# A residual stream handed on times the sublayer root, in a one-core encoder kernel

## The chip, the cores and the metric

The kernel runs on one core of a Trainium2 chip. The metric is the device time of one launch in microseconds (us), smaller is better. The core's engines are TensorE (PE, with its weight loads shown apart as PEld), VectorE (DVE), ScalarE (ACT), GpSimd (POOL) and the queue of SyncE (SP) that issues the weight transfers.

## The reference

The reference is a two-layer encoder trunk over 272 tokens (16 meta tokens and 256 real ones) of width 1024. Six sublayers follow one another: FFN, attention, FFN in layer 0, FFN, a gated recurrent block, FFN in layer 1. Each is wrapped in two RMS norms:

```python
def rms_norm(x, g):
    return x * rsqrt(mean(x * x, axis=-1) + 1e-6) * g

h = h + 0.5 * rms_norm(swiglu(rms_norm(h, g[0]), w_in, w_out), g[1])
h = h + rms_norm(mixer(rms_norm(h, g[2])), g[3])     # attention or recurrent block
h = h + 0.5 * rms_norm(swiglu(rms_norm(h, g[4]), w_in, w_out), g[5])
```

After the last sublayer the 256 real tokens are returned.

## The kernel before

**Layout.** The stream `h` lies transposed, as 8 chunks of 128 features by 272 tokens (256 from the recurrent block's output on, where the meta tokens are dropped). A dense product is made in three TensorE products of split numbers: high weights times high input, low times high, high times low. So `xh` (ACT, `x_high`, line 989) and `xl` (DVE, `low_x`, L1414) are the high and low parts of `h` times the norm's gain, and `wh` (ACT, `high`, L983) and `wl` (DVE, `low`, L1408) those of a weight unit of 128 x 2048. The norm's factor over features is a number for each token; it is put on the products' outputs, as `r` (L1423).

**Order.** Everything is written out by hand, one queue for each engine, with semaphores between them. Weight units go through four slots: SP loads a unit once its slot's `w_ready` has come, ACT makes `wh`, DVE makes `wl`, TensorE uses both.

**The boundary between two sublayers.** There are five, numbered here first to fifth by `pj` = 0 to 4. The output projection leaves 8 tiles in PSUM. ACT squares each (`square_tile`, L1015, into `sqb`) and copies it times the gain into `mg` (L1017). DVE adds the squares of tiles 0 to 5 into `acc` (L1431). Then:

- `mean_of_projection` (TensorE): three products with `acc` and three with each of the two last squares give the mean square of each token, with 96 tokens in partitions (L633). Three products keep the array warm (L482).
- `root_of_projection` (ACT, L1024): the root of 96 x 3 numbers. DVE takes their reciprocal (L1441). TensorE spreads them over 128 partitions with 3 products (`spread`, L521), into the PSUM tile `SUM_POST`.
- `residual` (DVE): for each chunk, `mg` times `SUM_POST` (L1446), `h` plus `mg` (L1450), and, one chunk behind, `xl` (L1414).
- ACT makes `xh` and the square `sqh` of each chunk (L989, L996) and GpSimd sums the squares in `hacc` (`sum_squares`: a copy for the first, L1914, and seven additions, L1917).
- TensorE begins the next sublayer with `chunk`: for each of 8 chunks of `h`, eight products with `xh` (L490, L491) as soon as that is there, then four with `xl` (L493).
- `mean_of_h` (L528) makes the mean square of the new `h` from `hacc`; root (L1006), reciprocal (L1419), `spread_r` (L521) and the copy into `r` follow.

After the recurrent block DVE makes one more weight unit's low part (`low(U_FFN[3] + 2, 0)`) between `residual` and the next sublayer's first step.

**At the start** DVE copies the eight turned chunks of the input out of PSUM (L1868) between the first halves of weight units (L1854), and then makes the eight `xl`.

**At the end** `turn_h` and `copy_h` (L668, L1128) turn `h` to token rows while the last FFN runs.

## Time and profile before

| | |
|---|---|
| median of 3 runs | 1066.18 us (1065.68 to 1066.78) |
| the profiled execution | 1066.7 us |
| its span from first to last instruction | 1064.9 us |
| PE, PEld busy | 99%, 96% of the span |
| DVE, ACT, POOL busy | 64%, 52%, 8% of the span |
| mean granted TensorE clock | 0.999 of full speed |
| chain that ended last | PE 92%, DVE 4%, ACT 2%, DMA 1% |

What lies around the span is 1.8 us. Matmuls overlap in the pipeline, so the duration of one is longer than the step to the next.

### The profile page before, as it was taken

To read this page: it belongs to the slowest core of one execution; us is meant where nothing else is said; L and a number is where in the kernel's file an instruction comes from. 1 tells how busy PE (TensorE), PEld (TensorE's weight loads), DVE (VectorE), ACT (ScalarE), POOL (GpSimd) and SP (SyncE) were. 2 spreads that over 40 slices of the span, in tenths; PEclk is the share of its full clock that TensorE was granted. 3 is DMA by queue.
4 is the path that set the end of the run, shared out by engine and by line. 5 is a ranking of instruction groups with operands and counts; after the bars stand their busy time and mean duration, and the time that the engine had idled before them with its cause. 6 is when DMAs were issued, how large, how long until landed. Compare 5 with 4: busy or idle time off the path is not lost.

```text
span 1064.9 us, 20573 instructions
## 1 busy us (share of the span) xinstructions
PE 1050.2 (99%) x8400; PEld 1022.3 (96%) x8400; DVE 686.2 (64%) x994; ACT 551.4 (52%) x806; POOL 81.2 (8%) x84
## 2 busy tenths in 40 slices
PE   9999999999999999999999999999999999999997
PEld 8999999999779999999999999999999999999986
DVE  6666656478865866654467666644798668667652
ACT  5444454457775644435455444444579755454541
POOL 0000000028000100000020000000234210000000
PEclk9999999999999999999999999999999999999999
DMA  9564446625204345535644554466328426646541
GB/s 309 174 211 158 138 147 205 222 90 171 69 2 159 119 159 164 190 130 181 205 159 160 190 165 138 134 207 210 101 86 271 159 81 203 193 158 208 190 135 40
DMA packets 160911, 170.16 MB, mean 160 GB/s; under 512 B 3264, under 2 KB 154104, under 8 KB 160840
## 3 DMA queue, kind: packets, MB, share of 16 engines
q1 hardware_dynamic: 160456, 168.70, 49.0%
q8 instruction: 51, 0.84, 0.3%
q0 software_dynamic: 96, 0.28, 0.1%
q10 hardware_dynamic: 288, 0.18, 0.1%
q14 instruction: 20, 0.16, 0.1%
HBM read 167.82 MB, written 1.05 MB: 159 GB/s over the span
## 4 chain that ended last, share of the span: by engine, by line
PE 92%; DVE 4%; ACT 2%; DMA 1%; issue 0%; SPq 0%; DVEq 0%; ACTq 0%
PE bank L474 23%; PE bank L476 23%; PE bank L475 23%; PE bank L884 5%; PE bank L682 2%; PE bank L681 2%; PE bank L683 2%; PE bank L493 1%; PE bank L490 1%; PE bank L491 1%; PE weighed L788 1%; DVE xl L1414 1%; PE flipped L776 1%; DVE h L1450 1%; DMA raw<-in_rec_w_in 1%; PE bank L521 1%
## 5 line engine op out<-in xcount | busy, mean ns | idle before, releaser
L1408 DVE TENSOR_TENSOR wl<-raw,wh 128x2048 fp32r<-128x2048 f32 (+2 forms) x164 | 339.2, 2090 | 152.5 <-ACT wh L983 152.2
L474 PE MATMUL bank<-xh,wl 128*128 128x272 f32 (+1 forms) x1488 | 430.6, 289 | 3.4 <-DVE tmp L1478 1.1
L476 PE MATMUL bank<-xh,wh 128*128 128x272 f32 (+1 forms) x1488 | 427.4, 287 | 0.0
L475 PE MATMUL bank<-xl,wh 128*128 128x272 f32 (+1 forms) x1488 | 425.9, 286 | 0.0
L983 ACT ACTIVATE wh<-raw 128x2048 fp32r<-128x2048 f32 (+2 forms) x164 | 282.2, 1744 | 104.6 <-PE bank L476 82.9
L474 PEld LDWEIGHTS bank<-xh,wl 128*128 128x128 f32 x1488 | 280.4, 188 | 5.2 <-issue 2.7
L476 PEld LDWEIGHTS bank<-xh,wh 128*128 128x128 f32 x1488 | 280.4, 188 | 0.0
L475 PEld LDWEIGHTS bank<-xl,wh 128*128 128x128 f32 x1488 | 280.3, 188 | 0.0
L474 PE MATMUL bank<-ah,wl 128*128 128x272 f32 x528 | 152.2, 288 | 0.0
L475 PE MATMUL bank<-al,wh 128*128 128x272 f32 x528 | 152.0, 288 | 0.0
L476 PE MATMUL bank<-ah,wh 128*128 128x272 f32 x528 | 151.6, 287 | 0.0
L1050 ACT ACTIVATE tmp<-tmp 128x272 f32<-128x272 f32 (+1 forms) x88 | 37.7, 428 | 215.3 <-DVE tmp L1477 215.0
L475 PEld LDWEIGHTS bank<-al,wh 128*128 128x128 f32 x528 | 99.4, 188 | 0.0
L474 PEld LDWEIGHTS bank<-ah,wl 128*128 128x128 f32 x528 | 99.3, 188 | 0.0
L476 PEld LDWEIGHTS bank<-ah,wh 128*128 128x128 f32 x528 | 99.2, 188 | 0.0
L1496 DVE TENSOR_TENSOR al<-tmp,ah 128x272 f32 (+3 forms) x88 | 38.2, 438 | 51.0 <-ACT ah L1055 50.6
L1477 DVE TENSOR_TENSOR tmp<-bank,r 128x272 f32<-128x272 f32 (+1 forms) x88 | 38.1, 433 | 49.9 <-PE bank L476 49.8
L1055 ACT ACTIVATE ah<-tmp 128x272 f32 (+3 forms) x88 | 37.4, 428 | 47.4 <-DVE tmp L1486 47.4
L1914 POOL COPY hacc<-sqh 128x272 f32<-128x272 f32 (+1 forms) x5 | 2.4, 484 | 706.9 <-ACT sqh L996 706.9
L490 PE MATMUL bank<-xh,wl 128*128 128x272 f32 (+1 forms) x176 | 46.0, 289 | 1.9 <-ACT xh L989 1.7
L1486 DVE TENSOR_TENSOR tmp<-tmp 128x272 f32<-128x272 f32 (+1 forms) x88 | 38.2, 437 | 14.0 <-ACT tmp L1050 10.8
L491 PE MATMUL bank<-xh,wh 128*128 128x272 f32 (+1 forms) x176 | 45.5, 287 | 0.0
(205 smaller groups left out, 1197.1 us busy)
## 6 DMA issues: line engine op xcount, KB each, us to landing
raw<-in_ffn_w_in SPq DMA_DIRECT2D x88, 1024.0 KB, 5.4
raw<-in_ffn_w_out SPq DMA_DIRECT2D x24, 768.0 KB, 4.3
raw<-in_ffn_w_out SPq DMA_DIRECT2D x24, 640.0 KB, 3.9
raw<-in_ffn_w_out SPq DMA_DIRECT2D x10, 1024.0 KB, 5.1
raw<-in_rec_w_in SPq DMA_DIRECT2D x8, 1024.0 KB, 5.7
raw<-in_attn_w_qkv SPq DMA_DIRECT2D x6, 1024.0 KB, 5.0
raw<-in_attn_w_o SPq DMA_DIRECT2D x4, 1024.0 KB, 5.6
raw<-in_rec_gate_w SPq DMA_DIRECT2D x16, 256.0 KB, 5.1
```

Of the source, the lines that this page charges most:

```text
L474: pe.matmul(dst, b, mh, start=first, stop=False)
L475: pe.matmul(dst, a, ml, start=False, stop=False)
L476: return pe.matmul(dst, a, mh, start=False, stop=last)
L490: pe.matmul(dst, b, xh[:, k, t0:L], start=k == 0, stop=False)
L491: pe.matmul(dst, a, xh[:, k, t0:L], start=False, stop=False)
L884: done = pe.matmul(dst[:, cols], w, x[:, cols], start=first and half == 0, stop=last, skip_group_check=True)
L983: act.activation(wh[:, slot(u), 0:kn * 256], raw[:, slot(u), 0:kn * 256], ACT.Copy).then_inc(wh_ready, units)
L1050: act.activation(sl[:, b, t0:L], gp[:, b, t0:L], ACT.Silu).then_inc(silu_done, 1)
L1408: dve.tensor_tensor(wl[:, slot(u), 0:kn * 256], w, wh[:, slot(u), 0:kn * 256].bitcast(F32), ALU.subtract).then_inc(w_ready, units)
L1477: dve.tensor_tensor(gp[:, b, t0:L], bank[banks[0]][:, t0:L], r[:, t0:L], ALU.mult).then_inc(gate_scaled, 1)
L1486: dve.tensor_tensor(aa[:, b, t0:L], sl[:, b, t0:L], up[:, b, t0:L], ALU.mult).then_inc(a_full, 1)
L1496: dve.tensor_tensor(d, aa[:, b, t0:L], s, ALU.subtract).then_inc(a_ready, 1)
```

## The change

Where a sublayer gave h + p/root (p the projection times its gain, root the root mean square of the projection), it now hands on h*root + p, which is root times the true stream. The next norm takes the factor out again, as long as its epsilon is multiplied by root squared; ACT puts that into `hacc` ahead of the squares (`hacc_set`). The steps:

- The mean square is made in all 128 partitions at once: `exact` products of 128x128 mean weights with `acc` and with the square of tile 7; DVE adds the square of tile 6 too (`ACC` = 9). ACT takes the root of 128 x 272 numbers straight out of PSUM into the SBUF tile `root`. The reciprocal and the spread between them and `residual` are gone. All 9 warming products stand behind.
- `residual` multiplies `h` by `root` (both in SBUF) and adds `mg`.
- Later, in the next sublayer's output projection, DVE inverts `root` (`invert_root`, 128 x 272 reciprocals), and GpSimd multiplies the 8 chunks of `h` by it (`restore`), before the next boundary uses `h`. Four sublayers do that; in the last the factor is put on by ACT's copy in `copy_h`, from `root_tok`, which `spread_r` and DVE make.
- `mean_of_h` moves into the products behind the chunks: for attention into tile 4 (k == 1), for the last FFN into its third tile (k == 2), with `spread_r` there from k == 3 to k == 6.
- GpSimd's first step of `sum_squares` is an addition in place of a copy.
- At the start ACT copies chunks 5 to 7 of `h`, and DVE makes two `xl` ahead of a weight half.

```diff
+EPS_SCALE = float(np.sqrt(D // P * EPS))
-        ACC = 8
+        ACC = 9
             def spread_r(n):
                 pe.wait_ge(rc_ready, n + 1)
+                if n == 5:
+                    for t in range(2):
+                        pe.matmul(SUM_PRE[:, SC + 3 + t:SC + 4 + t], root[:, META + t * P:META + (t + 1) * P], ident[:, 0:1], start=True, stop=True)
                 spread(SUM_PRE, rc_pre).then_inc(r_spread, 1)
-                if n:
+                if n in (1, 2):
                     mean_of_h(X_OF_FFN[n])
-                            if n == 0 and f == f0 + 2 and part == 0 and k == 7:
-                                mean_of_h(0)
-                            if f == f0 + 2 and (part, k) == ((0, 3) if n else (1, 6)):
+                            if f == f0 + 2 and (part, k) == {0: (0, 7), 3: (0, 2)}.get(n):
+                                mean_of_h(X_OF_FFN[n])
+                            if f == f0 + 2 and (part, k) == {0: (1, 2), 3: (0, 6)}.get(n, (0, 3)):
                                 spread_r(X_OF_FFN[n])
             def mean_of_projection(pj):
-                first = True
-                for ready, value, squares in ((acc_step, ACC * pj + ACC, acc[:, :]),
-                                              (sq_ready, 8 * pj + 7, sqb[:, 0, :]), (sq_ready, 8 * pj + 8, sqb[:, 1, :])):
-                    pe.wait_ge(ready, value)
-                    for c, a in enumerate(KTOK):
-                        last = pe.matmul(SUM_POST[0:KT, SC + c:SC + c + 1], squares[:, a:a + KT], mean_w,
-                                         start=first, stop=value == 8 * pj + 8, skip_group_check=True)
-                        first = False
-                last.then_inc(post_sum, 1)
-                idle_bank = bank[3] if pj == 4 else bank[5]
-                keep_warm(3, idle_bank)
-                pe.wait_ge(rt_ready, pj + 1)
-                spread(SUM_POST, rc_post).then_inc(rt_spread, 1)
-                keep_warm(6, idle_bank)
+                a, w = PROJ_T0[pj], mean_w.broadcast_to([P, P])
+                pe.wait_ge(acc_step, ACC * pj + ACC)
+                exact(SUM_POST[:, a:L], w, acc[:, a:L], True, False)
+                pe.wait_ge(sq_ready, 8 * pj + 8)
+                exact(SUM_POST[:, a:L], w, sqb[:, 1, a:L], False, True).then_inc(post_sum, 1)
+                keep_warm(9, bank[3] if pj == 4 else bank[5])
...
-                mean_of_h(1)
...
+                            if k == 1:
+                                mean_of_h(1)
...
             def root_of_projection(pj):
+                a = PROJ_T0[pj]
                 act.wait_ge(post_sum, pj + 1)
-                act.activation(rc_post[:, :], SUM_POST[0:KT, SC:SC + 3], ACT.Sqrt, bias=EPS).then_inc(post_root, 1)
+                if pj:
+                    act.wait_ge(h_restored, 8 * pj)
+                act.activation(root[:, a:L], SUM_POST[:, a:L], ACT.Sqrt, bias=EPS).then_inc(post_root, 1)
+                act.wait_ge(post_root, pj + 1)
+                act.wait_ge(pre_sum, pj + 1)
+                act.activation(hacc[:, a:L], root[:, a:L], ACT.Square, scale=EPS_SCALE).then_inc(hacc_set, 1)
...
+                act.wait_ge(root_inverted, 5)
+                act.activation(h_tok[:, t, 512 * half:512 * half + 512], bank[6][:, :], ACT.Copy, scale=root_tok[:, t:t + 1]).then_inc(h_turned_copied, 1)
...
+            def invert_root(n):
+                dve.wait_ge(hacc_set, n)
+                dve.reciprocal(root[:, PROJ_T0[n]:L], root[:, PROJ_T0[n]:L]).then_inc(root_inverted, 1)
             def residual(pj):
                 n, t0 = pj + 1, PROJ_T0[pj]
+                if pj:
+                    dve.wait_ge(h_restored, 8 * pj)
+                dve.wait_ge(mg_ready, 8 * pj + 8)
                 dve.wait_ge(post_root, pj + 1)
-                dve.reciprocal(rc_post[:, :], rc_post[:, :]).then_inc(rt_ready, 1)
-                dve.wait_ge(mg_ready, 8 * pj + 8)
-                dve.wait_ge(rt_spread, pj + 1)
                 def scale(c):
-                    dve.tensor_tensor(mg[:, c, t0:L], mg[:, c, t0:L], SUM_POST[:, t0:L], ALU.mult).then_inc(mg_scaled, 1)
+                    dve.tensor_tensor(h[:, c, t0:L], h[:, c, t0:L], root[:, t0:L], ALU.mult).then_inc(h_scaled, 1)
...
                 def group(g, it=0):
                     for j in range(3):
+                        if (g, j) == (3, 2):
+                            add_squares(pj, 6)
                         next_unit(g, j, it)
...
                 group(0)
+                if n:
+                    invert_root(X_OF_FFN[n])
...
             def projection(pj, u0):
                 for g in range(4):
+                    add_squares(pj, 2 * g)
                     if g < 3:
-                        add_squares(pj, 2 * g)
                         add_squares(pj, 2 * g + 1)
                         low(u0 + g + 4, 0)
+                    if g == 0:
+                        invert_root(pj)
                 residual(pj)
...
             def recurrent_out():
-                for m in range(6):
+                invert_root(4)
+                for m in range(7):
                     add_squares(4, m)
...
             def sum_squares(n):
-                pool.wait_ge(pre_sum, n)
-                if n == 2:
-                    pool.wait_ge(norm_q_sum, 1)
+                pool.wait_ge(hacc_set, n)
...
+            def restore(n):
+                t0 = PROJ_T0[n]
+                pool.wait_ge(root_inverted, n)
+                pool.wait_ge(x_ready, 8 * n + 8)
+                for c in range(KC):
+                    pool.tensor_tensor(h[:, c, t0:L], h[:, c, t0:L], root[:, t0:L], ALU.mult).then_inc(h_restored, 1)
```

`restore(1)` stands behind GpSimd's `rotary`, `restore(2)` and `restore(3)` behind `sum_squares` of their number, `restore(4)` behind GpSimd's part of the recurrent block.

## Rows read from the trace of the kernel before

**Rows 1.** Stretches: us, busy PE, PEld, DVE, ACT, POOL (instructions), clock, DMA share, GB/s

```profile
343.00:356.00 13.00, 12.64 (x99) 12.35 (x99) 11.00 (x22) 8.28 (x17) 6.29 (x8) 1.00 0.01 2
356.00:545.00 189.00, 189.00 (x1510) 189.00 (x1509) 113.85 (x135) 87.35 (x103) 0.00 (x0) 1.00 0.54 177
```

**Rows 2.** Timeline of the second boundary: start, duration, engine, line [idle before <-releaser]

```profile
338.67 0.59 PE L633 MATMUL bank<-cst,acc 128*96 128x1 f32 x6
338.86 0.40 ACT L1015 ACTIVATE sqb<-bank 128x272 f32<-128x272 f32 x1 [2.25 <-PE bank L476]
...
339.12 1.16 PE L633 MATMUL bank<-cst,sqb 128*96 128x1 f32 x12
...
340.31 0.17 ACT L1024 ACTIVATE rc_post<-bank 96x3 f32<-96x3 f32 x1 [0.67 <-PE bank L633]
...
341.80 0.44 DVE L1446 TENSOR_TENSOR mg<-mg,bank 128x272 f32<-128x272 f32 x1 [1.12 <-PE bank L521]
```

**Rows 3.** Timeline of DVE in its residual, second boundary

```profile
344.69 1.01 DVE L1414 SCALAR_TENSOR_TENSOR xl<-h,vec_a,xh 128x272 fp32r<-128x272 f32 x1
345.63 0.42 DVE L1446 TENSOR_TENSOR mg<-mg,bank 128x272 f32<-128x272 f32 x1
346.09 0.73 DVE L1450 TENSOR_TENSOR h<-h,mg 128x272 f32<-128x272 f32 x1
346.74 0.49 DVE L1414 SCALAR_TENSOR_TENSOR xl<-h,vec_a,xh 128x272 fp32r<-128x272 f32 x1
...
353.92 0.50 DVE L1414 SCALAR_TENSOR_TENSOR xl<-h,vec_a,xh 128x272 fp32r<-128x272 f32 x1 [0.18 <-ACT xh L989]
```

**Rows 4.** Timeline of GpSimd in the same stretch

```profile
343.75 0.47 POOL L1914 COPY hacc<-sqh 128x272 f32<-128x272 f32 x1 [75.49 <-ACT sqh L996]
344.50 0.90 POOL L1917 TENSOR_TENSOR hacc<-hacc,sqh 128x272 f32<-128x272 f32 x1 [0.28 <-ACT sqh L996]
345.73 0.78 POOL L1917 TENSOR_TENSOR hacc<-hacc,sqh 128x272 f32<-128x272 f32 x1 [0.33 <-ACT sqh L996]
...
354.28 0.78 POOL L1917 TENSOR_TENSOR hacc<-hacc,sqh 128x272 f32<-128x272 f32 x1 [1.26 <-ACT sqh L996]
```

**Rows 5.** Timeline of TensorE: its first chunk product and what follows the last

```profile
343.42 0.36 PE L490 MATMUL bank<-xh,wl 128*128 128x272 f32 x1 [0.35 <-ACT xh L989]
...
355.89 0.59 PE L528 MATMUL bank<-cst,hacc 128*96 128x1 f32 x6
```

**Rows 6.** Chain that ended last: the two halves of one exact fp32 product of 272 columns

```profile
236.43 0.34 PE bank L738 x2
236.76 0.23 PE bank L739 x2
```

**Rows 7.** DVE groups by shape: busy us, mean ns of one

```profile
L1677 DVE RECIPROCAL rinv<-rsum 128x2 f32<-128x2 f32 x16 | 2.6, 160 | 1.2 <-ACT prow L1233 1.1
...
L1832 DVE RECIPROCAL small<-small 128x16 f32<-128x16 f32 x1 | 0.3, 253 | 0.0
```

**Rows 8.** Timeline of DVE in the first FFN's projection

```profile
174.05 1.76 DVE L1408 TENSOR_TENSOR wl<-raw,wh 128x1536 fp32r<-128x1536 f32 x1 [0.23 <-DVE qg L1844]
```

**Rows 9.** Timeline of TensorE where the attention's chunks end

```profile
233.33 0.59 PE L528 MATMUL bank<-cst,hacc 128*96 128x1 f32 x6
234.25 0.36 PE L474 MATMUL bank<-xh,wl 128*128 128x272 f32 x1 [0.33 <-ACT tmp L1174]
```

**Rows 10.** Chain that ended last, behind the fifth boundary's last chunk

```profile
879.28 2.77 DVE wl L1408
882.09 0.39 PE bank L474
```

**Rows 11.** Timeline of TensorE at the kernel's start, before the second unit's tiles

```profile
20.09 0.39 PE L490 MATMUL bank<-xh,wl 128*128 128x272 f32 x1 [0.16 <-DVE wl L1854]
```

**Rows 12.** Timeline of DVE and ACT in the recurrent block's output projection

```profile
850.88 4.48 DVE L1408 TENSOR_TENSOR wl<-raw,wh 128x2048 fp32r<-128x2048 f32 x2
...
864.19 0.38 ACT L1348 ACTIVATE sqb<-bank 128x256 f32<-128x256 f32 x1 [1.04 <-PE bank L884]
```

More of the change, by code:

```diff
@@ L189, in build @@
         rc_pre = sb("rc_pre", [KT, 3])
-        rc_post = sb("rc_post", [KT, 3])
+        root = sb("root", [P, L])
+        root_tok = sb("root_tok", [P, 2])
         rsq = sb("rsq", [KT, 3])
@@ L278, in build @@
             "gu_done", "gate_scaled", "silu_done", "up_scaled", "a_full", "ah_ready", "a_ready"))
-        proj_done, sq_ready, mg_ready, acc_step, post_sum, post_root, rt_ready, rt_spread, mg_scaled = (sem(n) for n in (
-            "proj_done", "sq_ready", "mg_ready", "acc_step", "post_sum", "post_root", "rt_ready", "rt_spread", "mg_scaled"))
+        proj_done, sq_ready, mg_ready, acc_step, post_sum, post_root, h_scaled, hacc_set, root_inverted, h_restored = (sem(n) for n in (
+            "proj_done", "sq_ready", "mg_ready", "acc_step", "post_sum", "post_root", "h_scaled", "hacc_set", "root_inverted", "h_restored"))
         qk_done, q_squared, q_gained, q_sum, q_step, q_root, q_rot, q_partner, q_cos, q_sin, q_roped, q_spread, q_final = (sem(n) for n in (
@@ L1005, in root_of_h @@
                 act.wait_ge(pre_sum, n + 1)
-                act.activation(rc_pre[:, :], SUM_PRE[0:KT, SC:SC + 3], ACT.Sqrt, bias=EPS).then_inc(pre_root, 1)
+                act.activation(rc_pre[:, :], SUM_PRE[0:KT, SC:SC + 3], ACT.Sqrt, bias=0.0 if n else EPS).then_inc(pre_root, 1)
             def square_tile(pj, m, b, it=0):
@@ L1127, in copy_h @@
                 act.wait_ge(h_turned, i + 1)
-                act.activation(h_tok[:, t, 512 * half:512 * half + 512], bank[6][:, :], ACT.Copy).then_inc(h_turned_copied, 1)
+                act.wait_ge(root_inverted, 5)
+                act.activation(h_tok[:, t, 512 * half:512 * half + 512], bank[6][:, :], ACT.Copy, scale=root_tok[:, t:t + 1]).then_inc(h_turned_copied, 1)
             def last_out():
@@ L1198, in attention @@
                 act.wait_ge(norm_q_sum, 1)
-                act.activation(rc_q[:, :], SUM_PRE[:, SC + 3:SC + 8], ACT.Sqrt, bias=EPS).then_inc(norm_q_root, 1)
+                act.activation(rc_q[:, :], SUM_PRE[:, SC + 3:SC + 8], ACT.Sqrt).then_inc(norm_q_root, 1)
                 root(0)
@@ L1373, in _ @@
             for c in range(5, KC):
+                act.wait_ge(x_trans, c + 1)
+                act.wait_ge(h_ready, c)
+                act.activation(h[:, c, :], bank[4 + c % 4][:, 0:L], ACT.Copy).then_inc(h_ready, 1)
                 x_high(0, c)
@@ L1465, in ffn @@
                 r_of_h(X_OF_FFN[n])
+                if n == 3:
+                    dve.reciprocal(root_tok[:, :], SUM_PRE[:, SC + 3:SC + 5]).then_inc(root_inverted, 1)
                 if n == 0:
@@ L1875, in _ @@
             low_half(0, 0)
-            for c in range(5, KC):
-                copy_h(c)
+            dve.wait_ge(vec_ready, 1)
+            low_x(0, 0)
+            low_x(0, 1)
             low_half(0, 1)
-            dve.wait_ge(vec_ready, 1)
-            for c in range(KC):
+            for c in range(2, KC):
                 low_x(0, c)
@@ L1907, in sum_squares @@
                 t0 = PROJ_T0[n - 1]
-                pool.wait_ge(pre_sum, n)
-                if n == 2:
-                    pool.wait_ge(norm_q_sum, 1)
+                pool.wait_ge(hacc_set, n)
                 for c in range(KC):
                     pool.wait_ge(hsq_ready, 8 * n + c + 1)
-                    if c == 0:
-                        pool.tensor_copy(hacc[:, t0:L], sqh[:, 0, t0:L]).then_inc(hacc_step, 1)
-                    else:
+                    if c:
                         pool.wait_ge(hacc_step, 8 * n + c)
-                        pool.tensor_tensor(hacc[:, t0:L], hacc[:, t0:L], sqh[:, c % 2, t0:L], ALU.add).then_inc(hacc_step, 1)
+                    pool.tensor_tensor(hacc[:, t0:L], hacc[:, t0:L], sqh[:, c % 2, t0:L], ALU.add).then_inc(hacc_step, 1)
+            def restore(n):
[4 more added lines that the diff above has]
+                    pool.tensor_tensor(h[:, c, t0:L], h[:, c, t0:L], root[:, t0:L], ALU.mult).then_inc(h_restored, 1)
             def rotary():
@@ L1975, in _ @@
             rotary()
+            restore(1)
             sum_squares(2)
+            restore(2)
             sum_squares(3)
+            restore(3)
             sum_squares(4)
             recurrent()
+            restore(4)
             sum_squares(5)
```

2 lines of the change are left out of this document (1 added, 1 removed).

## Prediction

> **What bounds the kernel.** I read the stretches first. Inside a sublayer TensorE is busy all the time (189.00 of 189.00 us from 356 to 545 at clock 1.00, while DVE has 75 us and ACT 102 us free) [rows 1]. Nothing that DVE, ACT or GpSimd gain or lose there shows in the time, as long as TensorE's inputs come before they are due. The time can only move where TensorE waits: at the kernel's start and at the five boundaries. So I went through the second boundary on the timeline (first, third and fourth have the same steps and durations within 0.1 us), and then through what differs at the first and the fifth.
>
> A boundary has two parts. In the first a single chain runs: the last square ends at 339.26, TensorE's mean products (nine, done in order, so the last square waits behind the sums before it) at 340.28, ACT's root at 340.48, and after reciprocal and spread DVE's first multiply starts at 341.80 [rows 2]. I call that moment T0. It is 2.54 us after the last square. In the second part DVE feeds TensorE chunk by chunk. TensorE begins at T0 + 1.62 and ends at T0 + 14.09 [rows 5]. Its 96 products at 0.126 us each (189.00 us over 1510) are 12.1 us [rows 1], so it waits only 0.4 us inside. DVE's last `xl` ends at T0 + 12.62 [rows 3]: that is 1.58 us a chunk against TensorE's 1.51, so the two are nearly even, and whichever grows is the bound.
>
> **What the second part is made of.** Undisturbed, DVE's three operations start 0.46 (multiply to add), 0.36 (add to `xl`) and 0.42 us (`xl` to the next multiply) apart, 1.24 us a chunk. But some are stretched: the `xl` at 344.69 takes 1.01 us where the one at 346.74 takes 0.49, and the add at 346.09 takes 0.73 where others take 0.44 [rows 3]. Each stretched one begins while a GpSimd addition runs (344.50, 345.73) [rows 4]. GpSimd lets it go at 344.69 + 0.52 = 345.21 and at 346.09 + 0.29 = 346.38, about 0.65 us after its own start (0.71 in the first case, where GpSimd itself had to wait for the add before). The multiply at 345.63 was not stretched, and no multiply is: one of its inputs lies in PSUM. Over the boundary six additions cost DVE 3 x 0.52 + 3 x 0.29 = 2.4 us, and in every second chunk part of GpSimd's time passed under the multiply.
>
> **The change, part by part.**
>
> *The chain to T0.* The last square ends at the same time and TensorE can take it at once (+0.06). One exact product of 272 columns takes 0.34 + 0.23 = 0.57 us [rows 6]. ACT then makes the root of 128 x 272 out of PSUM: like its square of the same shape, 0.40 us [rows 2], plus 0.04 and 0.03 us from engine to engine. Sum: 0.06 + 0.57 + 0.04 + 0.40 + 0.03 = 1.10 us where it was 2.54: T0 comes 1.4 us earlier. Bounds: if the root took what an `xh` takes (0.52), 1.3; if it were as short as the old root (0.17), 1.65. The new add of tile 6 lies beside TensorE's last tile; where it stands before a 2.29 us `low`, that ends some 0.5 us before T0. ACT's square for `hacc` falls in the 0.95 us before the first `xh`.
>
> *The chunks.* The multiply is now `h` times `root`, two inputs in SBUF, like the add and the `xl`. I take it that it is held up as they are. The first GpSimd step becomes an addition too. I follow the queues with these rules: the starts above; a DVE operation on two SBUF inputs keeps GpSimd out for 0.30 us; GpSimd keeps DVE out for 0.65 us; GpSimd's addition is due 1.41 us after the start of the add of its chunk. For the old kernel this gives the last `xl` at T0 + 12.73 and TensorE's end at T0 + 14.14 (trace: 12.62 and 14.09). For the new one seven additions hold up, in turn, a multiply by 0.54, an add by 0.48, an `xl` by 0.59, an add by 0.56, and so on: 3.8 us in all. The `xl` end at T0 + 2.15, 4.41, 6.24, 7.96, 9.79, 11.51, 13.34, 13.75; TensorE needs chunk 6's (13.34) + 0.06, then 0.50 for its rest and 1.51 for chunk 7: T0 + 15.41. DVE is now the bound at 1.78 us a chunk, and this part is 1.3 us longer. Bounds: no hold-up of the multiply, 0.07; GpSimd keeping 0.75 in place of 0.65, 2.2. The net of a boundary is 1.3 - 1.4 = -0.1 us.
>
> The Trainium skill, "SBUF — State Buffer", section "Who interferes with whom", says that a DVE instruction with two SBUF inputs contends with a GpSimd instruction that reads SBUF, and one with at most one SBUF input does not. That is the line that the rows show between `mg` and the other two, and it speaks against this change.
>
> *Third, fourth and second boundary.* Three times -0.1: -0.3 us.
>
> *First boundary.* The next tile waits for ACT (`q_gained`) and starts at 234.25, and the mean products at 233.33 lie in that gap [rows 9]. The start moves forward by some 0.2 us, but the mean products now stand inside the tile, where TensorE is never idle: six passes of 0.09 us, +0.55. Net +0.35.
>
> *Fifth boundary.* TensorE waits for a low weight part that DVE makes behind its last `xl`, until 882.09 [rows 10]. That comes 1.4 earlier and 1.0 later: -0.4. The mean products stood in that wait and now cost 0.55; `spread_r` has two more products with `root` (four passes, 0.37). Net +0.5. The next unit's low part, behind the reciprocal of the later root, is due only 0.15 us after it is ready: cover that could go, at up to 0.5 us.
>
> *Start.* TensorE misses 0.33 us before 20.09, waiting for DVE's half unit [rows 11]. DVE loses three copies (1.13 us); ACT takes them and has 0.8 us to spare. -0.3.
>
> *Inverting and restoring.* From 2 to 16 elements a reciprocal grows from 160 to 253 ns, 6.6 ns each [rows 7]: 272 make an estimated 1.95 us, four times. In the first FFN a string of small DVE operations (3.7 us) at the same place made the next `low` late, at 174.05 [rows 8], and TensorE missed nothing there. So it costs nothing. Eight GpSimd multiplies follow, at 0.71 us or so (its additions take 0.78 with overlap [rows 4]), 5.7 us in projections of 19 to 65 us. Nearest to late is the fifth boundary: DVE is free at 855.36, the inverse done at 857.3, the eight done by 863.0, or 865.1 if all seven DVE adds hold them up by 0.3; ACT's root wants them at 865.3 [rows 12]. Cover there is 0.2 to 2.3 us. Without it each us late is a us lost.
>
> **Sum.** -0.3 (start) + 0.35 (first) - 0.3 (second to fourth) + 0.5 (fifth) = +0.25 us on the profiled execution's 1066.7 (span 1064.9 and 1.8 around it), which lies 0.5 us above the median of the runs, 1066.18. On the median: **1066.4 us, no change**. Own range 1064.1 to 1068.3.
>
> **Rivals.**
>
> *A. The multiply is hardly held up.* GpSimd may slip behind DVE's now unbroken row of two-input operations, or the lock may not bite on this form. Then the whole 1.4 us of each boundary is kept: -0.3 - 7.0 + 0.55 + 0.92 = -5.8, 1060.4; with half of the hold-up, 1063.6. For it: between multiply and `xl` the gap is longer (0.12 us) and GpSimd's sum is not urgent. Against: the add and the `xl`, of the same kind, were held every time. 27%.
>
> *B. The restored stream comes late at the fifth boundary* (slower). If a GpSimd multiply takes 1.0 us, as wide ones with contention do, and the seven adds hold it up, it ends at 857.3 + 8.0 + 2.1 = 867.4, 2.1 us late: 1068.5. It decides from 0.8 us a multiply on. Against: 0.71 was seen free of DVE. 11%.
>
> *C. A GpSimd addition shuts DVE out for its whole recorded 0.78 us.* The same hand working gives T0 + 16.48 for TensorE's end: +1.0 at each boundary, 1072. Against: 0.65 fits the rows of the old kernel to 0.1 us. 5%.
> The Trainium skill, same page and section, says that the one that comes second fully blocks for the whole instruction; by that C would be the outcome, and the trace so far agrees only in part (0.52 and 0.29 of delay, by when the operation came).
>
> **Chances.** Forecast 52%, A 27%, B 11%, C 5%, 5% for a stall not seen (a late weight part at 885, a slower reciprocal). 0.2% is 2.1 us, about what this kernel's runs can tell from no change. Faster by more: A and a little of the forecast, 0.28. Slower: B, C and the rest in part, 0.17. Same: 0.55. Range 1061.8 to 1068.9: it leaves out A's end and C.
>
> **What would show it.** In the new trace: DVE's first multiply 1.1 us after the last square's end (step 1). Multiplies of 0.43 us and, every second chunk, of 0.9 us, and 1.78 us a chunk (step 2); if all multiplies take 0.43, A holds. TensorE's first chunk product to its last 13.8 us in place of 12.5. One reciprocal near 1.95 us in each of four sublayers, TensorE still fully busy there. The last of eight GpSimd multiplies before ACT's root; if ACT waits for it, B. The forecast fails if GpSimd's additions pass under the DVE row or behind it.

## The result, and the profile after

The changed kernel takes 1067.69 us (median of 19 executions, 1066.35 to 1070.67) against 1066.19 us of the kernel before (19, 1065.30 to 1066.78): ratio 1.0018, 95% interval 1.0012 to 1.0024. The forecast was 1066.4, no change beyond 0.2%. The median is 1.3 us above it, inside the stated range. Six of the 19 lie at 1068.99 to 1070.67, and all six have a mean granted clock of 0.996 or 0.997, the others 0.998 to 1.000; the median of these other thirteen is 1067.11. The profiled execution took 1067.87 us (span 1066.0, before 1064.9).

Part 1 of the page (busy time, share of the span, instructions) says only that TensorE is still the bound; the other engines have room:

```profile
PE 1049.9 (98%) x8324; PEld 1017.2 (95%) x8324; DVE 703.8 (66%) x996; ACT 556.2 (52%) x814; POOL 120.7 (11%) x116
```

Where the time moved is read by laying both timelines side by side at points that both kernels have: the end of each boundary's last square, and TensorE's first product behind the fifth boundary.

| point | before | after | after - before |
|---|---|---|---|
| last square, first boundary | 216.68 | 215.05 | -1.63 |
| second | 339.26 | 337.93 | -1.33 |
| third | 544.89 | 543.49 | -1.40 |
| fourth | 750.54 | 749.03 | -1.51 |
| fifth | 864.57 | 863.99 | -0.58 |
| TensorE goes on behind the fifth | 882.09 | 882.12 | +0.03 |
| end of the span | 1064.9 | 1066.0 | +1.1 |

So 1.6 us were won before the first boundary, little moved from there to the fourth, 0.9 were lost between the fourth and the fifth, 0.6 at the fifth boundary and 1.1 behind it. The fourth boundary itself is not where the 0.9 went: from its last square to the mean products of `h` (L528 before, L530 after) both kernels take 16.6 us. They went in the recurrent block.

The first row holds some chance. TensorE's first product with `xh`:

```profile
13.67 0.37 PE L508 MATMUL bank<-xh,wl 128*128 128x272 f32 x1
...
13.90 0.37 PE L510 MATMUL bank<-xh,wl 128*128 128x272 f32 x1
```

It starts at 13.67 before and at 13.90 after, and in the profiles of all the kernels here anywhere from 12.60 to 14.03, whatever was changed. What makes it vary is open; it lies in the idle products at the very start, which take 5.7 to 7.2 us. Counted from this product the first boundary's last square comes after 203.01 us before and after 201.15 us after, and in each of the nine other profiles of kernels with the change after 201.14 or 201.15. So the change won 1.86 us there, and this one profile gave 0.23 of them back.

The timeline of the second boundary after, by engine (start, duration, engine, line; idle before it and who ended it in brackets), answers to [rows 2 to 5]:

```profile
337.53 0.40 ACT L1012 ACTIVATE sqb<-bank 128x272 f32<-128x272 f32 x1 [2.25 <-PE bank L478]
338.75 0.40 ACT L1024 ACTIVATE root<-bank 128x272 f32<-128x272 f32 x1 [0.44 <-PE bank L881]
...
338.00 0.71 PE L881 MATMUL bank<-sqb,cst 128*128 128x136 f32 x4
...
339.27 0.44 DVE L1458 TENSOR_TENSOR h<-h,root 128x272 f32<-128x272 f32 x1 [1.90 <-ACT root L1024]
...
341.35 1.02 DVE L1458 TENSOR_TENSOR h<-h,root 128x272 f32<-128x272 f32 x1
342.41 0.89 DVE L1462 TENSOR_TENSOR h<-h,mg 128x272 f32<-128x272 f32 x1
...
344.46 1.01 DVE L1421 SCALAR_TENSOR_TENSOR xl<-h,vec_a,xh 128x272 fp32r<-128x272 f32 x1
345.39 0.43 DVE L1458 TENSOR_TENSOR h<-h,root 128x272 f32<-128x272 f32 x1
345.86 0.91 DVE L1462 TENSOR_TENSOR h<-h,mg 128x272 f32<-128x272 f32 x1
...
344.25 0.91 POOL L1934 TENSOR_TENSOR hacc<-hacc,sqh 128x272 f32<-128x272 f32 x1 [1.25 <-ACT sqh L993]
345.50 0.96 POOL L1934 TENSOR_TENSOR hacc<-hacc,sqh 128x272 f32<-128x272 f32 x1 [0.33 <-ACT sqh L993]
...
354.56 0.59 PE L530 MATMUL bank<-cst,hacc 128*96 128x1 f32 x6
```

T0 is 339.27, 1.34 us after the last square (it was 2.54), TensorE's last chunk product ends at T0 + 15.29 (it was 14.09). Of the multiplies only the one at 341.35 is stretched, by 0.59, and the add behind it by 0.45. From there on each pair of chunks has one `xl` stretched by 0.52 and one add by 0.46; before, the add lost 0.29 [rows 3]. The seven additions of GpSimd hold DVE up by 3.5 us in all.

The restoring work, in the second boundary's sublayer (DVE's inverse, then GpSimd's eight multiplies), and ahead of the fifth boundary:

```profile
324.49 1.85 DVE L1447 RECIPROCAL root<-root 128x272 f32<-128x272 f32 x1
...
326.42 10.67 POOL L1942 TENSOR_TENSOR h<-h,root 128x272 f32<-128x272 f32 x8 [59.49 <-DVE root L1447]
...
856.57 6.69 POOL L1942 TENSOR_TENSOR h<-h,root 128x256 f32<-128x256 f32 x8 [10.20 <-DVE root L1447]
```

The eight end at 337.09 and the root wants them at 338.75; at the fifth boundary [rows 12] they end at 863.26, wanted at 864.80. Cover is 1.5 to 1.7 us. One multiply takes 1.33 us on average in the second boundary's sublayer and 0.84 ahead of the fifth boundary, waits included.

Two things that the prediction did not have. In the first FFN of the kernel before, TensorE waited 1.11 us because DVE got `r` only at 33.36:

```profile
34.84 0.39 PE L474 MATMUL bank<-xh,wl 128*128 128x272 f32 x1 [1.11 <-DVE tmp L1478]
...
33.36 0.44 DVE L1423 COPY r<-bank 128x272 f32<-128x272 f32 x1 [3.02 <-PE bank L521]
```

After, `spread_r(0)` stands four chunks earlier, DVE's copy starts at 31.64 and TensorE waits nowhere there. And at the fifth boundary [rows 10] ACT has a weight unit between the root (864.80) and the first `xh` (timeline after, ACT and then TensorE):

```profile
865.53 1.90 ACT L980 ACTIVATE wh<-raw 128x2048 fp32r<-128x2048 f32 x1
867.34 0.49 ACT L986 ACTIVATE xh<-h,vec_a 128x256 fp32r<-128x256 f32 x1
...
867.97 0.36 PE L492 MATMUL bank<-xh,wl 128*128 128x256 f32 x1 [1.20 <-ACT xh L986]
882.12 0.38 PE L476 MATMUL bank<-xh,wl 128*128 128x256 f32 x1 [1.26 <-DVE wl L1415]
883.29 0.59 PE L530 MATMUL bank<-cst,hacc 128*96 128x1 f32 x6
885.25 0.50 PE L537 MATMUL bank<-cst,root 128*128 128x1 f32 x4
```

Before, the unit ran from 865.71 to 867.61, most of it in the 1.5 us from ACT's root to T0, and the first `xh` followed at 868.04, 0.91 after T0. Now the first `xh` starts 2.03 us after T0, directly behind the unit. The shorter chain leaves it no room.

### The profile page after: what moved, and what is told of

It reads as the page before. It is cut to its first block, busy times and chain, and to the rows that moved or that the text cites. A ratio compares the mean times of both kernels' runs of the same rounds, so it can differ in the third digit from the quotient of the medians.

```text
span 1066.0 us, 20492 instructions
## 1 busy us (share of the span) xinstructions
PE 1049.9 (98%) x8324; PEld 1017.2 (95%) x8324; DVE 703.8 (66%) x996; ACT 556.2 (52%) x814; POOL 120.7 (11%) x116
## 4 chain that ended last, share of the span: by engine, by line
PE 93%; DVE 4%; ACT 2%; DMA 1%; issue 0%; SPq 0%; DVEq 0%; ACTq 0%
PE bank L476 23%; PE bank L478 23%; PE bank L477 23%; PE bank L881 5%; PE bank L495 2%; PE bank L679 2%; PE bank L678 2%; PE bank L680 2%; PE bank L492 1%; PE bank L493 1%; PE weighed L783 1%; DVE h L1462 1%; PE flipped L771 1%; DMA raw<-in_rec_w_in 1%; DVE h L1458 1%; DVE xl L1421 1%
## 5 line engine op out<-in xcount | busy, mean ns | idle before, releaser
L1415 DVE TENSOR_TENSOR wl<-raw,wh 128x2048 fp32r<-128x2048 f32 (+2 forms) x164 | 342.9, 2113 | 140.0 <-ACT wh L980 139.7
L478 PE MATMUL bank<-xh,wh 128*128 128x272 f32 (+1 forms) x1488 | 427.4, 287 | 0.0
L1942 POOL TENSOR_TENSOR h<-h,root 128x272 f32<-128x272 f32 (+1 forms) x32 | 35.2, 1134 | 360.5 <-DVE root L1447 360.5
L1934 POOL TENSOR_TENSOR hacc<-hacc,sqh 128x272 f32<-128x272 f32 (+1 forms) x40 | 36.3, 907 | 329.3 <-ACT sqh L993 328.6
```

What stands on the lines that cost most here:

```text
L478: return pe.matmul(dst, a, mh, start=False, stop=last)
L1415: dve.tensor_tensor(wl[:, slot(u), 0:kn * 256], w, wh[:, slot(u), 0:kn * 256].bitcast(F32), ALU.subtract).then_inc(w_ready, units)
```

## The experiments

Each kernel was timed beside the kernel before on the same chip; medians of before were 1066.08 (first four), 1065.76 (next four) and 1066.18 (last three).

**1. One part alone, in the kernel before.**

```
-  if f == f0 + 2 and (part, k) == ((0, 3) if n else (1, 6)):
+  if f == f0 + 2 and (part, k) == ((0, 3) if n else (1, 2)):
       spread_r(X_OF_FFN[n])
```

> The kernel before with one thing of the change: in the first FFN the spread of r stands behind chunk 2 of its tile in place of chunk 6. Theory (the missed gain of the changed kernel lies here): TensorE's wait of 1.11 us at 34.84 for DVE's scaled gate goes, the last square of the first boundary ends at 215.0 in place of 216.28, and each boundary up to the fourth is 1.2 earlier. Behind the recurrent block 0.5 to 1.2 of it are left, as far as a weight unit there lands no earlier: median 1065.0 to 1065.7. Rival: the earlier spread only moves the wait (r waits for ACT's root instead), first boundary within 0.2 of before, median 1066.2.

1065.21 us, ratio 0.9987 (0.9978 to 0.9996). The last squares of the first four boundaries are 1.00 to 1.03 earlier, that of the fifth 0.54: between them TensorE now waits 0.67 us at 841.91 for a `rout_x` transfer. But this profile's first product with `xh` starts at 14.02, 0.35 later than before; counted from it, the first boundary's last square comes 1.36 earlier (201.65 in place of 203.01). The theory holds, with 1.36 for the 1.2 expected. A part of the change that the prediction passed over was its largest gain. The other 0.50 of the 1.86 come from the rest that differs ahead of the first boundary, mainly the start.

**2. The root in PSUM for the multiply.** The change of `root_of_projection` and `scale`:

```
+  act.activation(SUM_PRE[:, a:L], SUM_POST[:, a:L], ACT.Sqrt, bias=EPS).then_inc(post_root, 1)
   act.activation(root[:, a:L], SUM_POST[:, a:L], ACT.Sqrt, bias=EPS).then_inc(root_set, 1)
...
-  dve.tensor_tensor(h[:, c, t0:L], h[:, c, t0:L], root[:, t0:L], ALU.mult)
+  dve.tensor_tensor(h[:, c, t0:L], h[:, c, t0:L], SUM_PRE[:, t0:L], ALU.mult)
```

> The changed kernel, but ACT makes the root twice: into a free PSUM bank, which DVE's multiplies read, and into SBUF for hacc, the inverse and the restoring. So the multiply has one input in SBUF and one in PSUM, as in the kernel before; all else is as changed. Theory (GpSimd's additions hold up DVE's operations on two SBUF inputs, and the multiply is one of them now): no multiply over 0.5 us, DVE's last xl at T0 + 12.7 in place of 13.55 at the second boundary, TensorE's last chunk product at T0 + 14.1 in place of 15.3, so 1.2 less at each of the five boundaries. Of the four ahead of the recurrent block most is lost again to the late weight unit there, so the median is 1065.0 to 1066.5; if nothing there were pinned it would be 1061.7. Rival: the hold-up only moves to add and xl (each over 0.9 every time), period stays at 1.73 us a chunk, stage as long as in the changed kernel, median 1067.7 or, with ACT's second root (0.4 us) in front of the first xh, 1068 to 1069.

1063.68 us (8 executions), ratio 0.9972 (0.9962 to 0.9983), below the expected 1065.0 to 1066.5. Second boundary, DVE, GpSimd and then TensorE; T0 is 337.01:

```profile
343.29 1.02 DVE L1422 SCALAR_TENSOR_TENSOR xl<-h,vec_a,xh 128x272 fp32r<-128x272 f32 x1
344.24 0.42 DVE L1459 TENSOR_TENSOR h<-h,bank 128x272 f32<-128x272 f32 x1
344.70 0.70 DVE L1463 TENSOR_TENSOR h<-h,mg 128x272 f32<-128x272 f32 x1
...
344.33 0.77 POOL L1935 TENSOR_TENSOR hacc<-hacc,sqh 128x272 f32<-128x272 f32 x1 [0.32 <-ACT sqh L993]
...
351.24 0.59 PE L530 MATMUL bank<-cst,hacc 128*96 128x1 f32 x6
```

TensorE ends at T0 + 14.23: 1.06 us less, where 1.2 was expected, and from one boundary to the next (first to second, and so on to the fourth) it gains 0.94, 1.08 and 1.04 us on the changed kernel. From the fourth to the fifth it loses 1.24: TensorE waits 2.16 us there for ACT's gates and goes on at the lower clock (as in run 4). The `xl` is stretched as before. What the PSUM operand saves is the one multiply's 0.59 and 0.44 in the adds (1.38 in three stretched adds with the root in SBUF, 0.94 in four with it in PSUM). So the multiply on two SBUF operands costs in two ways: it is held up itself, and it holds GpSimd up, whose addition beside it takes 0.96 in place of 0.77 so that the add behind it pays (0.91 in place of 0.70).

**3. ACT's unit moved.**

```
       act.activation(mg[:, m, t0:L], rout_dst(m), ACT.Copy, scale=...).then_inc(mg_ready, 1)
+      if m == 5:
+          high(U_FFN[3] + 2, 0)
   root_of_projection(4)
-  high(U_FFN[3] + 2, 0)
```

> The changed kernel, but at the fifth boundary ACT's high half of the weight unit (1.90 us) stands behind the square and gain of tile 5 in place of behind the root. Theory: in the changed kernel it stands on the path between root and the first xh (867.34); without it the first xh starts at 866.3, DVE's last xl and its low part behind it end 1.0 earlier, TensorE's wait at 882.12 ends at 881.1, and the median is 1066.7. Rival 1: the unit now makes the square of tile 6 late by 0.9 and tile 7's with it, so the boundary starts later and nothing is won (1067.7). On the spread: executions of the changed kernel at 1069 to 1070.7 have a mean granted clock of 0.996 to 0.997, those at 1066.4 to 1068.1 one of 0.998 to 1.000. If TensorE's idle 1.20 us ahead of 867.97 is what lets the clock fall, these are gone here (all within 1.5 us of each other) and the median falls by more, to 1066.2; if it lies elsewhere, about one in three stays 3 us above the others.

1066.47 us, ratio 1.0001 (0.9992 to 1.0010). From the fifth boundary's last square (863.88) TensorE goes on 17.01 us later, in the changed kernel 18.13: the 1.0 us is confirmed. Counted from the square of tile 5, that of tile 6 is 0.65 us late, that of tile 7 is not.

```profile
880.89 0.39 PE L476 MATMUL bank<-xh,wl 128*128 128x256 f32 x1 [0.99 <-DVE wl L1416]
```

One of 11 executions (1067.90) still has a clock of 0.997 although the idle 1.20 us is gone, so that idle can't be the only place where the clock falls.

**4. Nothing inverted or restored.** `restore` does no multiplies, `invert_root` no reciprocal.

> The changed kernel without the four 128-partition reciprocals and GpSimd's 32 multiplies that restore h: h stays multiplied by the roots, so the outputs are other numbers, all else stands. Theory: both are hidden, TensorE is busy all through the FFNs and the projections, and the last restoring multiply is done 1.5 us before it is due: median within 0.3 of the changed kernel, boundaries at the same times within 0.2. Rival: the stretched low parts and additions of DVE (up to 2.39 us beside GpSimd in place of 2.1) make TensorE's weights late or delay the chain at the fifth boundary: 0.5 to 1.5 us less.

1068.28 us, ratio 1.0023 (1.0014 to 1.0032). The first four boundaries are at the times of the changed kernel within 0.04. The restoring is hidden; rival B is out. Five of 11 executions have a clock of 0.997, and the profiled one is one of them. The stretches from 810 on (TensorE busy, its loads, DVE, ACT, GpSimd, then granted clock, DMA share, GB/s), and TensorE's row:

```profile
810.00:812.00 2.00, 0.16 (x1) 0.16 (x2) 1.97 (x4) 1.99 (x4) 1.30 (x1) 1.00 0.79 251
812.00:814.00 2.00, 2.00 (x15) 2.00 (x16) 2.00 (x3) 1.39 (x4) 1.02 (x1) 0.83 0.04 14
814.00:816.00 2.00, 2.00 (x11) 2.00 (x10) 1.97 (x3) 0.49 (x1) 0.38 (x1) 0.50 0.00 0
816.00:818.00 2.00, 2.00 (x16) 2.00 (x15) 2.00 (x2) 0.96 (x2) 0.00 (x0) 0.82 0.00 0
...
811.84 5.64 PE L881 MATMUL bank<-xc,raw 128*128 128x136 f32 x32 [2.02 <-ACT gr L1277]
```

The clock goes to 0.50, the lower of its two levels (1.2 GHz), behind a wait of 2.02 us, and the 32 passes take 5.64 us where the changed kernel's profile has 3.97. From the fourth boundary's last square to the fifth's it is 2.04 us more than in the changed kernel's profile, about the whole difference between the two profiled executions (1069.79 and 1067.87). So this execution loses its time in the recurrent block, behind TensorE's wait for ACT's gates. That the six long executions of the changed kernel lose theirs there too is likely but not shown: none of them was profiled. Why is this wait 1.72 us in the changed kernel's profile and 0.69 before?

**5. The instruction fetch.** ACT starts those gates late because the weight unit `e3` lands late. Rows before and after: the issue of the `e2` unit (the first of the transfers in the queue), that of `e3`, ACT's use of `e3`, TensorE's wait; then what had moved from the first issue to the landing.

```profile
796.48 0.37 SPq L434 DMA_DIRECT2D raw<-in_rec_w_in  x1
...
799.38 0.47 SPq L434 DMA_DIRECT2D raw<-in_rec_w_in  x1
...
808.33 1.91 ACT L983 ACTIVATE wh<-raw 128x2048 fp32r<-128x2048 f32 x1 [0.40 <-DMA raw<-in_rec_w_in]
...
812.18 3.97 PE L884 MATMUL bank<-xc,raw 128*128 128x136 f32 x32 [0.69 <-ACT gr L1275]
...
DMA packets 3527, 3.51 MB, mean 298 GB/s; under 512 B 96, under 2 KB 3527, under 8 KB 3527
```

```profile
794.84 0.37 SPq L436 DMA_DIRECT2D raw<-in_rec_w_in  x1
...
797.54 0.47 SPq L436 DMA_DIRECT2D raw<-in_rec_w_in  x1
...
807.75 1.91 ACT L980 ACTIVATE wh<-raw 128x2048 fp32r<-128x2048 f32 x1 [1.79 <-DMA raw<-in_rec_w_in]
...
811.60 3.97 PE L881 MATMUL bank<-xc,raw 128*128 128x136 f32 x32 [1.72 <-ACT gr L1279]
...
DMA packets 3951, 3.96 MB, mean 309 GB/s; under 512 B 96, under 2 KB 3950, under 8 KB 3950
q8 instruction: 1, 0.02, 7.0%
```

`e2`, the gate pieces and `e3` are 3.15 MB. Before, 3.51 MB had moved when `e3` was there, after 3.96: the surplus belongs to later transfers. The reading is that some of the 16 DMA engines had gone on to them while another still had its part of `e3` to do; no row shows a single engine, so this step is inferred. The last line (of the microsecond from 802) names what it did: one packet of 0.02 MB of queue 8, instructions, 7.0% of 16 engines for 1 us, so 1.12 us of one engine. In the kernel before these fetches lie at 794 and 811, outside the stretch. The change took 8 products from TensorE's stream at each boundary (13 in place of 21), 128 instructions over four with their two passes and weight loads, and so moved the fetches along the code. (At one pass and its weight load each 0.126 us, 128 instructions are an estimated 8 us, which is the step from 794 to 802.)

The edit puts 36 products back, as twice as many of half the width, at hardly any time (0.06 to 0.13 us from one boundary to the next):

```
-  keep_warm(9, bank[3] if pj == 4 else bank[5])
+  if pj < 4:
+      for _ in range(18):
+          pe.matmul(bank[5][:, 0:P // 2], ident, ident[:, 0:P // 2], start=True, stop=True)
+  else:
+      keep_warm(9, bank[3])
```

> The changed kernel, but at the first four boundaries the 9 idle products of 128 columns behind the mean are 18 of 64 columns: TensorE's instruction stream gets 36 products (144 instructions with their two passes and weight loads) longer, its time there stays the same to 0.3 us. What it tests: in the changed kernel, in all four traces of its family so far, an instruction fetch of 0.02 MB takes 1.1 us of one DMA engine (at 802) between the issue of the e2 weight unit (794.84) and the landing of e3 (807.68), by which 3.9 to 4.05 MB have moved; in the kernel before and its twin with the early spread the fetches lie outside (794 and 811) and 3.4 to 3.5 MB have moved. Theory: that fetch makes the one engine late and e3 lands 1.2 us later; with the longer stream it lies outside again, e3 lands 8.7 to 9.0 us after its issue in place of 10.1, ACT waits 0.5 us for it in place of 1.8, TensorE 0.6 for ACT's gate in place of 1.7, no execution has a mean clock under 0.998, and the median falls from 1067.7 to 1066.0 to 1066.6. Rival: the late landing comes from something else of the changed kernel (its root tile shifts all addresses; GpSimd's and DVE's use of SBUF): landing stays at 10.1, median 1067.7.

1066.07 us, ratio 1.0003 (0.9994 to 1.0012). The fetches are at 791 and 808, `e3` is issued at 797.21:

```profile
805.95 1.91 ACT L984 ACTIVATE wh<-raw 128x2048 fp32r<-128x2048 f32 x1 [0.39 <-DMA raw<-in_rec_w_in]
...
809.80 3.97 PE L885 MATMUL bank<-xc,raw 128*128 128x136 f32 x32 [0.34 <-ACT gr L1283]
```

ACT has the unit 8.7 us after its issue in place of 10.2, and TensorE's wait is 0.34 in place of 1.72 (0.6 was expected). So the place of the fetch decides when `e3` lands; the rival, that it lands late for another cause in the changed kernel, is out. One of 11 executions still has a clock of 0.997 (1067.39), which the theory had excluded.

**6. `e3` issued ahead of the gate pieces.**

```
-  for j, what in enumerate(REC_ORDER):
+  for j in (*range(10), 11, 10):
+      what = REC_ORDER[j]
```

> The changed kernel, but SP issues the e3 unit ahead of the four gate pieces of g3, which are needed later. Theory: e3 then has 1 MB less in front of it and lands 3 us earlier, ACT waits for no weight unit there, TensorE's 1.72 us ahead of 811.60 go, the fifth boundary comes 1.7 to 1.9 earlier, none of the executions has a clock under 0.998, median 1065.6 to 1066.0. Rival: ACT's own row (table loads, square roots) or g3 coming late takes the place: at most 0.5 won.

1066.06 us, ratio 1.0001 (0.9992 to 1.0010), all executions within 1.2 us and none under 0.998, with a fetch at 801 inside the stretch as in the changed kernel. ACT does not wait for the transfer any more, TensorE waits 0.26 us. Counted from the first boundary's last square, the fifth comes 1.3 us earlier than in the changed kernel, less than the 1.7 expected, and the median is at the upper end of the expected 1065.6 to 1066.0.

**7. TensorE kept busy in the wait.** 7 idle products before gate 20's `wait_ge(sig_done, ...)`, behind a `wait_ge(e_scaled, 2)` of their own.

> The changed kernel, but TensorE makes 7 idle products (14 passes of 0.12 us, 1.7 us) in the stretch in which it waits for ACT's gates in the recurrent block (809.9 to 811.6). The wait stays, only TensorE is not idle in it. Theory: what the slow third of the executions (1069 to 1070.7, mean clock 0.996 to 0.997) loses is the clock that falls to half behind that wait, as the trace of the kernel without the restoring shows at 813 to 817: here no execution has under 0.998, all lie within 1.8 us of each other, median 1067.0 to 1067.5. Rival: the clock falls elsewhere (start, fifth boundary): about one in three stays at 1069 to 1071.

1067.87 us, ratio 1.0020 (1.0011 to 1.0029). One of 11 executions has a low clock (1069.76, 0.996) where the changed kernel had six of 19; the rest spread over 1066.56 to 1068.81, more than expected, and the median lies above the expected 1067.0 to 1067.5. Fewer long executions point to the idle stretch but don't prove it; the median did not move.

**8. The means of h back at their old places.**

```
   (attention, behind the chunks)
+  mean_of_h(1)
   (last FFN)
-  if n in (1, 2):
+  if n:
       mean_of_h(X_OF_FFN[n])
```

and the spread of `r` in the last FFN behind chunk 3 again.

> The changed kernel with the mean products of h back at their old places in the attention (behind the chunks) and the last FFN (behind the first tiles, with the spread of r behind chunk 3 of its tile; the two products with root stay). Theory of the prediction: each stood in a wait of TensorE before and costs 0.55 us inside a tile, so 0.3 us are won at the first boundary and 0.55 at the fifth: median 1066.8. Rival: at the old places TensorE now waits for GpSimd's last addition (it ends 0.8 us after DVE's last xl) and for ACT's root right behind, so nothing is won, 1067.7 or more.

1066.38 us, ratio 1.0003 (0.9994 to 1.0012). From the first boundary's last square to the second's 122.34 us, in the changed kernel 122.88: 0.54 won, more than 0.3. From the fifth's to the end 201.4 against 202.0: 0.6. The term of 0.55 stands. One of 11 executions has a clock of 0.997 (1067.88).

**9. Without GpSimd's additions.**

```
+  if c:
+      pool.sem_inc(hacc_step, 1)
+  else:
       pool.tensor_tensor(hacc[:, t0:L], hacc[:, t0:L], sqh[:, c % 2, t0:L], ALU.add)
```

> The changed kernel with 7 of GpSimd's 8 additions of the squares of h left out at every boundary, so the mean square of h is too small and the outputs are other numbers; root stays in SBUF. Theory (the additions are what stretches DVE's row): DVE's three operations take 1.24 us a chunk, TensorE becomes the bound and ends at T0 + 14.0 to 14.1 in place of 15.3, the last xl at T0 + 10.5 to 12.5. Ahead of the recurrent block that is 1.2 us at each of three boundaries more than in the changed kernel, as with the root in PSUM (339.26 - 335.68); median 1062.5 to 1064.5, with the clock lost behind the longer wait in the recurrent block in some executions. Rival: DVE's row is longer for another cause (ACT's xh late, SBUF reads of DVE and ACT): stage stays over T0 + 14.8.

1059.00 us (5 executions), ratio 0.9932 (0.9918 to 0.9946), below the expected range. Second boundary, T0 337.65:

```profile
342.79 0.43 DVE L1458 TENSOR_TENSOR h<-h,root 128x272 f32<-128x272 f32 x1
343.26 0.44 DVE L1462 TENSOR_TENSOR h<-h,mg 128x272 f32<-128x272 f32 x1
343.62 0.49 DVE L1421 SCALAR_TENSOR_TENSOR xl<-h,vec_a,xh 128x272 fp32r<-128x272 f32 x1
...
351.40 0.59 PE L530 MATMUL bank<-cst,hacc 128*96 128x1 f32 x6
```

1.24 us a chunk, TensorE ends at T0 + 13.75. GpSimd's additions thus cost the changed kernel 1.54 us a boundary, and the one with the root in PSUM 0.48. From the first to the fourth boundary's last square that makes 4.6 us, where the expectation had 1.2 at each of three boundaries. The fourth gives 1.5 too, but the profile loses them again in the recurrent block (a wait of 1.92 us, then the lower clock), and behind the fifth's last square 2.9 us are won, because DVE's `xl` and the low part behind them end earlier and TensorE's wait of 1.26 us goes.

**10 and 11. All of it together, and the same without the change.** `all_mended` is the changed kernel with edits 2, 3, 6 and the attention half of 8; besides, DVE's low part of the fifth boundary's unit stands ahead of the residual. `before_mended` is the kernel before with edits 1, 3, 6 and that low part.

> The changed kernel with four things mended together: the multiply reads the root from PSUM, ACT's weight unit of the fifth boundary stands behind tile 5 and DVE's low part of it ahead of the residual, e3 is issued ahead of g3, and the first boundary's mean of h stands where it stood before the change. Theory by the single runs: -3.0 (multiplies, second to fourth boundary) -1.0 (fifth) -1.2 (ACT's unit) -0.7 (low part ahead) -1.8 (e3) -0.3 (mean) from 1067.7: 1059.0 to 1061. Rival: with the boundaries shorter another transfer or a low part of DVE becomes late, and it stays above 1062.

> The kernel before with what the experiments found beside the change: r spread early in the first FFN, the e3 unit issued ahead of g3, ACT's weight unit of the fifth boundary behind tile 5 and DVE's low part of it ahead of the residual. What it tells: what the change itself (h times the root, restored later, root in PSUM) is worth when both kernels have the rest. Theory: -1.0 (spread) -0.7 (e3: ACT waits 0.40 for it) -0.9 to -1.3 (low part ahead; TensorE's wait at 882) from 1066.1: 1063.0 to 1063.6, so the shorter chain (1.2 us less from last square to T0) is worth the other 4.5 to 5 us to 1058.7. Rival: the mends are worth as much in the kernel before as the change, 1060 or less, and the change itself is worth under 2 us.

1058.67 us (5 executions), ratio 0.9929 (0.9916 to 0.9943), and 1063.56 us (11), ratio 0.9976 (0.9967 to 0.9985); the first is just below its expected range of 1059.0 to 1061, the second inside its own. At the fifth boundary of `all_mended` TensorE waits only here; the wait of 1.26 us at 882 is gone:

```profile
861.09 0.35 PE L493 MATMUL bank<-xh,wl 128*128 128x256 f32 x1 [0.23 <-ACT xh L986]
```

Between the two, the change with its root in PSUM is worth 4.9 us. The spans differ by as much (1056.9 and 1061.8), and by stage it is 1.14, 1.16 and 1.14 us from one last square to the next up to the fourth, 1.06 to the fifth, and 0.57 behind it. That is about 1 us a boundary. The low part ahead of the residual was not run alone, and the two kernels still differ in small things (the copies at the start, the mean products in the last FFN), so the 4.9 are those of the whole change.

## Why the prediction was right, and where it was not

*The chain to T0*: forecast 1.10 us after the last square, measured 1.34. The exact product was put at 0.57 and takes 0.71, the step from ACT to DVE at 0.03 and is 0.12 (339.15 to 339.27). Right in mechanism, 0.24 off in size.

*The chunks*: forecast TensorE's end at T0 + 15.41, measured 15.29; period 1.78, measured 1.73. The row worked out came out operation by operation: the `xl` end at T0 + 2.16, 4.44, 6.20, 7.91, 9.66, 11.36 and, the last, 13.55, each within 0.2 us of its forecast. Seven additions hold up a multiply by 0.59, an add by 0.45 and then `xl` and add in turn by 0.52 and 0.46, 3.5 us in all where 3.8 was forecast. Counted from GpSimd's recorded start it keeps DVE out for 0.73 us (`xl`) and 0.83 (add); without the 0.14 and 0.19 for which it was itself held up (0.91 and 0.96 us for 0.77), that is 0.59 and 0.64, where the working had 0.65. What was wrong is the sign named under "What would show it", a multiply of 0.9 in every second chunk: the working's own steps of 1.83 and 1.72 us have only the first multiply held up, and so has the trace. Rival A, no hold-up, is thus nearly true of the multiplies and false for the time; C is out (15.29, not 16.48).

By the Trainium skill, "SBUF — State Buffer", section "Who interferes with whom", an operation of DVE with at most one SBUF input, outside the two-port modes, doesn't contend with GpSimd. Run 2 agrees: no multiply there is over 0.44 us, and GpSimd's addition beside it takes 0.77 in place of 0.96. The same section calls the lock exclusive and says, of the two-port modes, that the second one is blocked for the whole instruction. The rows come near that without reaching it: the `xl` at 344.46 came with 0.70 us of GpSimd's recorded time left and was 0.52 late, the add at 345.86 with 0.60 left and 0.47 late.

*Second to fourth boundary*: from last square to last square -0.07 for the second and -0.11 for the third, forecast -0.1 each; the fourth is -0.03 up to the mean products of `h`. *First boundary*: +0.30, forecast +0.35. *Inverting and restoring*: 1.85 us for 1.95, and multiplies of 0.84 to 1.33 us for 0.71. The forecast let rival B decide from 0.8 on; it didn't, since the eight at the fifth boundary began at 856.57 and took 6.69 us in all, inside the forecast's 5.7 to 7.8. Hidden (run 4).

*Start*: forecast -0.3, measured -1.63 by the first boundary, or -1.86 counted from TensorE's first product with `xh`. The step that failed is that only the half unit was followed: `spread_r(0)` was moved too, past a wait of 1.11 us that stood in the trace. Worth 1.36 us (run 1); the forecast's own part measured 0.50.

*Fifth boundary*: forecast "1.4 earlier and 1.0 later: -0.4", measured +0.6 up to 882 [rows 10]. The chain was shortened onto ACT's weight unit, whose cover was the old chain; 1.1 us (run 3). The products behind it came as forecast: 0.55 + 0.37 = 0.92, measured 1.07.

*Recurrent block*: forecast nothing, measured +0.96 in the profile; the 2 to 3 us of the third of the executions at a low clock are probably lost there too. A fetch of instructions makes `e3` land late (run 5). The working looked at the products removed only as time, not as instructions.

The misses were -1.3 (start), +1.2 (fifth) and +1.0 (fourth boundary and recurrent block). They sum to +0.9, which with the forecast 0.25 is the span's 1.1. The forecast held since they nearly cancelled, not because its sum was complete: that is luck. On the median 1.5 us were measured for 0.2 forecast; 0.6 of them hang on the six executions at a low clock, without which the median is 1067.11.

## What to carry to other kernels

When a chain is shortened, list what each engine did inside its old gaps: that work is now on the path. Of an operation that goes from one SBUF operand to two, ask whom it keeps out as well as who holds it up; a copy of the shared operand in PSUM cost 0.4 us of an idle ACT here and gave back a microsecond a boundary. Where a transfer has under 1 us of cover, issue it ahead of transfers that are due later, since gains ahead of it and the place of instruction fetches decide whether it lands in time.

## What the runs showed of the hardware

A fetch of instructions (0.02 MB, one packet) takes 7.0% of 16 DMA engines for 1 us, that is 1.12 us of one of them, and a weight transfer that is in flight lands about that much later (from the issue of `e3` to ACT's use of it 9.9 to 10.4 us in the profiles of the seven kernels in the old order of issue with the fetch inside, 8.5 to 9.0 in three with it outside). Its place goes with the number of TensorE's instructions, loads included (802 in the changed kernel, 791 and 808 with 144 instructions more, run 5).

Waits of TensorE of 1.92, 2.02 and 2.16 us in the recurrent block were followed by the lower clock level in the profiles of three kernels (runs 9, 4 and 2); waits of 0.26 to 1.78 in the profiles of the others were not. One execution in 11 of runs 3, 5, 7 and 8 shows a low clock all the same, and was not profiled: where it fell there stays open.
